# Queries and keys of the last eight heads ahead of their values, and stick-breaking steps one half later

## The chip, the cores and the metric

The kernel runs on one core of a Trainium2 chip. The metric is the device time of one execution in microseconds; times are medians of several executions, and one execution was profiled.

## The reference

Two layers of a hybrid encoder over 256 tokens of width 2048, in float32. Cut to what matters here:

```
xn   = rms_norm(x)
proj = xn @ w_in                        # 16 heads of 128: q, k, v, and 5 forget columns
a: softmax(q1 k1) - lam * softmax(q2 k2), q and k normed in halves of 64, distance bias   (6 heads)
b: stick-breaking: a = exp(log_sigmoid(z) + sum of log_sigmoid(-z) to the right), strict  (5 heads)
c: softmax(q k + cumulated log forget), q and k normed                                    (5 heads)
x    = x + concat(rms_norm(a), rms_norm(b), rms_norm(c)) @ w_out
x    = x + experts(rms_norm(x))         # 16 experts, top 2 within the best of 4 groups
```

## The kernel before, in words

All engines run long programs of their own, in order, and meet at semaphores. The attention part of a layer is one stream of weights: 96 halves of the input projection and 32 of the output projection (a half is 1024 columns times 128 rows of weights, 12 matmuls; eight halves make a block of 512 output columns). The matmuls work on a sum of two reduced-precision parts. For half n ScalarE writes the high part wh (cut, L522), VectorE the low part wl (cut, L1091), and TensorE does xh·wh, xh·wl and xl·wh (L775 to L777). There are four buffers of wh and wl: the cut of half n + 3 begins when TensorE is through with half n - 1.

The attention of the 16 heads is threaded between the halves. Heads go in the order a b c a b c ... a. Tables made from one row of numbers, TURN, say after which half each step of a head stands: turn (transposes of queries and keys, L826), one half later query (to SBUF) and scores (L844 to L854), then SOFT (row_max, or stick_scores on ScalarE with its table load), EXPS, WEIGH (weigh or stick_keep, VectorE, L1255 to L1260), MIDDLE (transposes of the weights, or the cumulated sum of a stick-breaking head, L869 to L878), BACK and SUMMED, STICK (stick_weights, L1272), OUTPUT (weights times values, L892 and L894) and OUT (ScalarE copies and squares, L606, L607). At step n each engine first does its cut of half n + 3 (TensorE: half n itself) and then the steps that the tables give to n, VectorE in the order to_proj (L1197), stick_weights, stick_sum, head_norms, turned_lo, row_max, stick_keep or weigh, out_norms. TensorE's order at a step is output, middle, scores, turn, mixed group.

When a block of eight halves is done, to_proj (first step of the next block) copies it to proj; one step later ScalarE squares the queries and keys in it (head_squares, L623), two steps later VectorE norms them (head_norms: a chain of small operations from L1099 and a scaling at L1144). A turn waits for the norms of its block. out_norms does the same to a pair of head outputs; the mixed groups (turn_group, L789, with turned_hi at L534 and turned_lo at L1128) transpose them for the output projection. In the last four heads the columns stand in another order: all their queries and keys, then all their values, and their outputs come at steps 96 to 99.

Of the kernel before, what the change touches and what calls it, by code (L numbers as in the profile page):

```python
# [24 lines left out]
P = 128  # L25
D, SEQ, DEPTH = 2048, 256, 2
NT = SEQ // P
NC = D // P
HD = 128
NH = D // HD  # L30
# [34 lines left out]
NORMS = NORM_AT[NH]  # L65
LATE = NH - 4
Q_AT = [3 * HD * i if i < LATE else 3 * HD * LATE + 2 * HD * (i - LATE) for i in range(NH)]
K_AT = [q + HD for q in Q_AT]
V_AT = [3 * HD * i + 2 * HD if i < LATE else 3 * HD * LATE + HD * (8 + i - LATE) for i in range(NH)]
SPAN = P + SEQ  # L70
# [28 lines left out]
NORMED = {j: [i for i in range(NH) if QK_BLOCK[i] == j and KIND[i] != "b"] for j in range(IN_UNITS // 4 - 1)}  # L99
TURN = dict(zip((19, 23, 27, 31, 36, 43, 51, 55, 59, 67, 75, 79, 83, 86, 90, 92), range(NH)))  # L100
BEGIN = {i: n for n, i in TURN.items()}


def steps_at(after, late=None):

    at = {}
    for i, n in BEGIN.items():
        n += after[KIND[i]] if isinstance(after, dict) else after
        if late is not None and i >= LATE:
            n = late + i - LATE  # L110
        at.setdefault(n, []).append(i)
    return at
# [5 lines left out]
WEIGH = steps_at(4)  # L118
MIDDLE = steps_at(5)
BACK = steps_at({"a": 6, "b": 7, "c": 6})  # L120
SUMMED = steps_at(6)
STICK = steps_at(8)
OUTPUT = steps_at({"a": 6, "b": 8, "c": 6}, IN_HALVES)
OUT = steps_at({"a": 7, "b": 9, "c": 7}, IN_HALVES + 1)
PAIR = {max(n for n, h in OUT.items() if 2 * g in h or 2 * g + 1 in h) + 1: g for g in range(NH // 2)}
MIXED = {91: 0, 92: 1, 93: 2, 94: 3, 97: 4, 98: 5, 100: 6, 101: 7}
MIX_BANK = (0, 1, 0, 1, 2, 3, 2, 3)
# [166 lines left out]
def trunk(nc, x_in, in_units, forget_w, out_units, expert_units, norms, small_in, const_in, router_in,  # L294
          rows_dram, picks_dram, out):
    with ExitStack() as ctx:
# [31 lines left out]
        rx = sb("rx", [P, NT])  # L328
        gains = sb("gains", [P, 2, NC])
        out_stat = sb("out_stat", [P, 3, NT, NH])  # L330
        more = sb("more", [1, 2])
# [24 lines left out]
        def sml(name):  # L356
# [16 lines left out]
                   for b in range(2)]  # L373
        weights = [wT[:, i % 2, :] if i < NH - 2 else proj[:, i % 2, 0:SPAN] for i in range(NH)]
        squares = wide[:, 4 * SPAN:4 * SPAN + NT * 2 * HD]
        turned_qk_bank, score_bank, middle_bank = bank[4], (bank[5], bank[6]), bank[7]
        out_bank = [(middle_bank if i < LATE else turned_qk_bank)[:, 0:NT * HD] for i in range(NH)]
        turned_w = wT[:, :, :].rearrange("p a n -> p (a n)")
# [130 lines left out]
        def _(e):  # L509
# [39 lines left out]
            with t_.layers():  # L549
# [38 lines left out]
                def turned(i):  # L588
                    if KIND[i] == "b":
                        e.wait_ge(S["sum_ready"], t_.due("sum_ready"))  # L590
                        act_(score[:, i % 2, 1, :], score[:, i % 2, 1, :], ACT.Exp).then_inc(S["a_ready"], 1)
                        return
                    e.wait_ge(S["m_banked"], t_.by("m_banked", i + 1))
                    if 2 <= i < NH - 2:

                        e.wait_ge(S["o_banked"], t_.by("o_banked", i - 1))
                    act_(weights[i], middle_bank[:, 0:SPAN], ACT.Copy).then_inc(S["wT_ready"], 1)

                def output(i):
                    e.wait_ge(S["o_banked"], t_.by("o_banked", i + 1))  # L600
                    if KIND[i] == "c":
                        e.wait_ge(S["sums_ready"], t_.due("sums_ready"))
                    for t in range(NT):
                        scale = soft[:, i % 3, 3, 2 * t:2 * t + 1] if KIND[i] == "c" else 1.0
                        o = out_bank[i][:, t * HD:(t + 1) * HD]
                        act_(rows[:, t, i * HD:(i + 1) * HD], o, ACT.Copy, scale=scale)  # L606
                        last = act_(o, o, ACT.Square, scale=scale,  # L607
                                    accum_out=out_stat[:, 0, t, i:i + 1])
                    last.then_inc(S["o_ready"], 1)
# [17 lines left out]
                def during(n):  # L627
# [25 lines left out]
                    for i in steps(TURN, n - 1):  # L653
                        query(i)
                    if n - 1 in MIXED:
                        turned_hi(MIXED[n - 1], mix_gain, MIX_BANK[MIXED[n - 1]])
                    for i in EXPS.get(n, ()):
# [109 lines left out]
        def _(e):  # L767
# [114 lines left out]
            def output(i):  # L882
                at, w = V_AT[i], weights[i]
                if i == LATE:

                    e.wait_ge(S["block_out"], t_.ahead("block_out", 1))
                if KIND[i] == "b":
                    at_least("aT_ready", KIND[:i + 1].count("b"))
                else:
                    at_least("wT_ready", i + 1 - KIND[:i].count("b"))  # L890
                at_least("o_ready", i)
                mm(out_bank[i][:, 0:HD], w[:, 0:P], proj[:, 0, at:at + HD], start=True, stop=True)  # L892
                for u in range(NT):
                    last = mm(out_bank[i][:, HD:2 * HD], w[:, (1 + u) * P:(2 + u) * P],  # L894
                              proj[:, u, at:at + HD], start=(u == 0), stop=(u == 1))
                last.then_inc(S["o_banked"], 1)
# [80 lines left out]
            with t_.layers():  # L977
# [42 lines left out]
                for n in range(4, HALVES):  # L1020
# [12 lines left out]
                    for i in steps(TURN, n):  # L1033
                        turn(i)
                    if n in MIXED:
                        g = MIXED[n]
                        at_least("mix_scaled", g + 1)
# [45 lines left out]
        def _(e):  # L1083
# [78 lines left out]
            with t_.layers() as layer:  # L1162
# [104 lines left out]
                def stick_weights(i):  # L1267
                    e.wait_ge(S["a_ready"], t_.due("a_ready"))
                    if i >= 2:

                        at_least("o_banked", i - 1)
                    v.tensor_tensor(weights[i], score[:, i % 2, 1, :], strict, ALU.mult).then_inc(S["aT_ready"], 1)  # L1272
# [34 lines left out]
                def weigh(i):  # L1307
                    b, m = i % 2, i % 3
                    e.wait_ge(S["exps_ready"], t_.due("exps_ready"))
                    if KIND[i] == "c":  # L1310
                        v.reciprocal(soft[:, m, 3, 0:3:2], soft[:, m, 2, 0:3:2]).then_inc(S["sums_ready"], 1)
                        return
# [15 lines left out]

                def out_norms(g):

                    at_least("o_ready", 2 * g + 2)
                    k = slice(2 * g, 2 * g + 2)
                    inverse_root(out_stat, 2 * g, 2 * g + 2, {HD: (2 * g, 2 * g + 2)})
                    for t in range(NT):
                        ins = scaled_heads(rows[:, t, 2 * g * HD:(2 * g + 2) * HD], out_stat[:, 2, t, k], 2)
                    ins.then_inc(S["mix_scaled"], 1)
                    if g == NH // 2 - 1:

# [3 lines left out]
                def during(n):  # L1342
# [24 lines left out]
                    if n % 8 == 2 and n // 8 - 1 in NORMED:  # L1367
                        head_norms(n // 8 - 1)
                    if n - 1 in MIXED:
                        turned_lo(MIXED[n - 1], mix_gain, MIX_BANK[MIXED[n - 1]])  # L1370
                    for i in SOFT.get(n, ()):
                        if KIND[i] != "b":
                            row_max(i)
                    for i in WEIGH.get(n, ()):
                        if KIND[i] == "b":
                            stick_keep(i)
                        else:
                            weigh(i)
                    for g in steps(PAIR, n):
                        out_norms(g)  # L1380
                    if n > HALVES - 8 and n - HALVES + 7 < 6:
# [302 lines left out]
```

## Time and profile before

| | us |
|---|---|
| median of 3 runs | 2129.95 (2129.71 to 2131.52) |
| the profiled execution | 2122.7 |
| its span, first to last instruction | 2121.0 |
| TensorE, VectorE, ScalarE busy | 1884.9, 1597.2, 1436.7 |
| mean granted clock of TensorE | 0.954 |

Each layer has three parts: the two projections with the attention between their halves, the routing, and the experts. A busy time is a sum over the span, so it mixes these parts; the tables of windows tell them apart. A clock of 1.00 is 2.4 GHz, 0.50 is 1.2 GHz. "[4.40 <-DVE proj L1144]" behind a row means that the engine was idle for 4.40 us before it, and that VectorE's instruction at L1144 ended the wait.

### The profile page before, as it was taken

Reading aid. Unit: us, or ns where it says so; the run is one execution under the profiler, and the core shown is the slowest. Engines: PE = TensorE matmul, PEld = TensorE weight load, DVE = VectorE, ACT = ScalarE, POOL = GpSimd, SP = SyncE. Lnnn points to the kernel's source line nnn. Section 1 sums busy time; section 2 is a strip of 40 time slices with the busy share of each in tenths; the row PEclk is TensorE's granted clock in tenths of the full one; section 3 lists DMA queues with packets and bytes.
Section 4 is the critical chain, followed back from the end, with each engine's and each line's share of the span. In section 5 each row is a group of like instructions: output and inputs, shape, how many; then the busy total and the mean of one; then the engine's idle time right before and its main releaser. Section 6 shows DMA issues by size and latency. Waiting matters only on the chain.

```text
span 2121.0 us, 31136 instructions
## 1 busy us (share of the span) xinstructions
PE 1884.9 (89%) x8974; PEld 1484.9 (70%) x8974; DVE 1597.2 (75%) x2301; ACT 1436.7 (68%) x2278; POOL 92.2 (4%) x86
## 2 busy tenths in 40 slices
PE   7999998995999999999489999989869999999993
PEld 6877776784677777677377777767757777677772
DVE  5567676546999999999464676665579999999993
ACT  5555555433888988989355555654448988988982
POOL 0000000001000000000000000000010000000000
PEclk9999999996999999999789999999879999999996
DMA  6434343454999999999534344435569999999993
GB/s 259 159 139 158 142 158 119 175 203 151 394 398 405 402 400 413 396 408 407 230 141 141 138 159 152 153 115 188 189 210 407 404 403 404 402 406 397 405 381 138
DMA packets 83005, 575.14 MB, mean 271 GB/s; under 512 B 11760, under 2 KB 12016, under 8 KB 13264
## 3 DMA queue, kind: packets, MB, share of 16 engines
q1 hardware_dynamic: 75600, 542.01, 66.0%
q0 software_dynamic: 7296, 31.85, 4.3%
q8 instruction: 48, 0.79, 0.2%
q14 instruction: 61, 0.50, 0.1%
HBM read 567.52 MB, written 23.07 MB: 278 GB/s over the span
## 4 chain that ended last, share of the span: by engine, by line
PE 64%; ACT 11%; issue 11%; DVE 9%; DMA 3%; ACTq 1%; DVEq 0%; POOLq 0%; POOL 0%; SPq 0%
PE bank L775 9%; PE bank L777 9%; PE bank L776 9%; PE bank L940 6%; ACT wh L522 6%; PE bank L924 6%; PE bank L942 6%; PE bank L941 6%; PE bank L926 5%; DVE wl L1091 3%; PE bank L907 2%; ACT rows L719 2%; PE bank L915 1%; DMA proj<-picks 1%; ACT wT L706 1%
## 5 line engine op out<-in xcount | busy, mean ns | idle before, releaser
L1091 DVE TENSOR_TENSOR wl<-raw,wh 128x1024 fp32r<-128x1024 f32 x640 | 767.7, 1222 | 325.8 <-ACT wh L522 324.9
L522 ACT ACTIVATE wh<-raw 128x1024 fp32r<-128x1024 f32 x640 | 664.3, 1054 | 407.4 <-PE bank L777 341.0
L1091 DVE TENSOR_TENSOR wl<-proj,wh 128x1024 fp32r<-128x1024 f32 x384 | 455.3, 1221 | 46.6 <-ACT wh L522 46.1
L924 PE MATMUL bank<-wh,xh 128*128 128x512 f32 x1024 | 428.0, 418 | 32.4 <-DVE wl L1091 29.4
L522 ACT ACTIVATE wh<-proj 128x1024 fp32r<-128x1024 f32 x384 | 394.5, 1052 | 66.5 <-PE bank L942 50.1
L775 PE MATMUL bank<-wh,xh 128*128 128x512 f32 x1024 | 418.8, 409 | 5.8 <-DVE xl L1128 3.1
L926 PE MATMUL bank<-wl,xh 128*128 128x512 f32 x1024 | 405.9, 396 | 0.0
L777 PE MATMUL bank<-wh,xl 128*128 128x512 f32 x1024 | 404.2, 395 | 0.0
L776 PE MATMUL bank<-wl,xh 128*128 128x512 f32 x1024 | 403.7, 394 | 0.0
L924 PEld LDWEIGHTS bank<-wh,xh 128*128 128x128 f32 x1024 | 194.3, 190 | 120.2 <-DVE wl L1091 80.6
L775 PEld LDWEIGHTS bank<-wh,xh 128*128 128x128 f32 x1024 | 195.8, 191 | 49.1 <-DVE wl L1091 9.5
L777 PEld LDWEIGHTS bank<-wh,xl 128*128 128x128 f32 x1024 | 194.9, 190 | 43.6
L776 PEld LDWEIGHTS bank<-wl,xh 128*128 128x128 f32 x1024 | 195.8, 191 | 37.0
L926 PEld LDWEIGHTS bank<-wl,xh 128*128 128x128 f32 x1024 | 194.9, 190 | 34.1
L940 PE MATMUL bank<-wh,actT 128*128 128x512 f32 x512 | 209.7, 410 | 3.6 <-DVE actT L1527 3.6
L942 PE MATMUL bank<-wh,actT 128*128 128x512 f32 x512 | 203.2, 397 | 0.0
L941 PE MATMUL bank<-wl,actT 128*128 128x512 f32 x512 | 203.2, 397 | 0.0
L940 PEld LDWEIGHTS bank<-wh,actT 128*128 128x128 f32 x512 | 96.8, 189 | 38.4 <-DVE wl L1091 11.2
L942 PEld LDWEIGHTS bank<-wh,actT 128*128 128x128 f32 x512 | 96.8, 189 | 23.1
L941 PEld LDWEIGHTS bank<-wl,actT 128*128 128x128 f32 x512 | 97.1, 190 | 19.7
L915 PEld LDWEIGHTS bank<-const,wT 128*128 128x128 f32 x512 | 66.1, 195 | 43.7 <-ACT wT L706 40.3
L915 PE MATMUL bank<-const,wT 128*128 128x64 f32 x512 | 69.1, 279 | 27.3 <-ACT wT L706 27.3
(209 smaller groups left out, 1539.0 us busy)
## 6 DMA issues: line engine op xcount, KB each, us to landing
raw<-in_expert_units SPq DMA_DIRECT2D x192, 1024.0 KB, 9.2
proj<-in_expert_units SPq DMA_DIRECT2D x192, 1024.0 KB, 9.4
raw<-in_in_units SPq DMA_DIRECT2D x96, 1024.0 KB, 4.8
raw<-in_out_units SPq DMA_DIRECT2D x32, 1024.0 KB, 4.8
proj<-picks POOLq DMA_DIRECT2D x8, 1024.0 KB, 8.1
expert_rows<-rows POOLq DMA_DIRECT2D x4, 1024.0 KB, 4.3
x<-in_x SPq DMA_DIRECT2D x2, 1024.0 KB, 6.4
wide<-in_norms POOLq DMA_DIRECT2D x2, 1024.0 KB, 5.3
```

The source lines that it names most:

```text
L522: act_(wh[:, h % CUT, :], ring[j][:, h % 2 * HALF:(h % 2 + 1) * HALF], ACT.Copy)\
L719: ins = act_(expert_out[b][:, k * COLS:(k + 1) * COLS], bank[2 + k][0:SLOTS, :], ACT.Copy, scale=slots[0:SLOTS, bass.ds(n, 1), 2:3].rearra ...
L775: mm(out, xh[:, at, tok], rh, start=start, stop=False)
L776: mm(out, xh[:, at, tok], rl, start=False, stop=False)
L777: return mm(out, xl[:, at, tok], rh, start=False, stop=stop)
L915: last = mm(bank[6][:, at + k * SLOTS:at + (k + 1) * SLOTS], wide_act[:, k * P:(k + 1) * P], cst("fold"), start=True, stop=True)
L924: mm(bank[m][:, :], stacked[b][:, 2 * h + c, :], wh[:, j, k], start=(h + c == 0), stop=False)
L926: last = mm(bank[m][:, :], stacked[b][:, 2 * h + c, :], wl[:, j, k], start=False, stop=(h == PART - 1 and c == 1))
L940: mm(o, actT[:, k, 0:STACK], wh[:, j, r], start=(k == 0), stop=False)
L941: mm(o, actT[:, k, 0:STACK], wl[:, j, r], start=False, stop=False)
L942: last = mm(o, actT[:, k, SLOTS:SLOTS + STACK], wh[:, j, r], start=False, stop=(k == 3))
L1091: v.tensor_tensor(wl[:, h % CUT, :], ring[(first + h // 2) % slots][:, h % 2 * HALF:(h % 2 + 1) * HALF], wh[:, h % CUT, :].bitcast(F32), A ...
```

## The change

LATE goes from NH - 4 to NH - 8: the columns of the last eight heads (8 to 15) now stand as their queries and keys first and then their values, in blocks 10 and 11. TURN is another row of numbers: heads 2 and 8 are turned one half later, heads 9 to 15 between four and eight halves earlier. The middle, sum, weights and output of a stick-breaking head come one half later after its turn. The outputs of heads 8 to 15 come at steps 89, 90, 91, 92, 96, 96, 97 and 97; their weights lie in dead columns of proj until then, and their outputs go to banks 4 to 7. The inverse sums of the forgetting heads get a tile of their own, inv_sum. out_norms can take several pairs, and pairs 6 and 7 go together, as do their mixed groups (step 100). In the table of steps:

| | before | after |
|---|---|---|
| turn of heads 0 to 7 | 19 23 27 31 36 43 51 55 | 19 23 28 31 36 43 51 55 |
| turn of heads 8 to 15 | 59 67 75 79 83 86 90 92 | 60 63 67 71 75 78 84 87 |
| block of q and k, heads 8 to 15 | 6 7 8 8 9 9 10 10 | 6 6 7 7 8 8 9 9 |
| middle, stick_weights and output of a stick head, after its turn | 5, 8, 8 | 6, 9, 9 |
| out_norms of pairs 0 to 7 | 33 39 51 65 75 87 99 101 | 34 39 51 66 92 94 99 99 |

```diff
-LATE = NH - 4
+LATE = NH - 8
-V_AT = [3 * HD * i + 2 * HD if i < LATE else 3 * HD * LATE + HD * (8 + i - LATE) for i in range(NH)]
+V_AT = [3 * HD * i + 2 * HD if i < LATE else 3 * HD * LATE + HD * (2 * (NH - LATE) + i - LATE) for i in range(NH)]
-TURN = dict(zip((19, 23, 27, 31, 36, 43, 51, 55, 59, 67, 75, 79, 83, 86, 90, 92), range(NH)))
+TURN = dict(zip((19, 23, 28, 31, 36, 43, 51, 55, 60, 63, 67, 71, 75, 78, 84, 87), range(NH)))
+LATE_OUTPUT = (89, 90, 91, 92, 96, 96, 97, 97)
...
-            n = late + i - LATE
+            n = LATE_OUTPUT[i - LATE] + late
...
-MIDDLE = steps_at(5)
-BACK = steps_at({"a": 6, "b": 7, "c": 6})
-SUMMED = steps_at(6)
-STICK = steps_at(8)
-OUTPUT = steps_at({"a": 6, "b": 8, "c": 6}, IN_HALVES)
-OUT = steps_at({"a": 7, "b": 9, "c": 7}, IN_HALVES + 1)
-PAIR = {max(n for n, h in OUT.items() if 2 * g in h or 2 * g + 1 in h) + 1: g for g in range(NH // 2)}
-MIXED = {91: 0, 92: 1, 93: 2, 94: 3, 97: 4, 98: 5, 100: 6, 101: 7}
+MIDDLE = steps_at({"a": 5, "b": 6, "c": 5})
+BACK = steps_at({"a": 6, "b": 8, "c": 6})
+SUMMED = steps_at(7)
+STICK = steps_at(9)
+OUTPUT = steps_at({"a": 6, "b": 9, "c": 6}, 0)
+OUT = steps_at({"a": 7, "b": 10, "c": 7}, 1)
...
+PAIR[max(PAIR)] = [6, 7]
+PAIR = {n: (g[0], g[-1] + 1) for n, g in PAIR.items() if g != [6]}
+MIXED = {91: (0,), 92: (1,), 93: (2,), 94: (3,), 97: (4,), 98: (5,), 100: (6, 7)}
...
-        weights = [wT[:, i % 2, :] if i < NH - 2 else proj[:, i % 2, 0:SPAN] for i in range(NH)]
+        weights = [wT[:, i % 2, :] if i < LATE
+                   else proj[:, i % 2, (i - LATE) // 2 * SPAN:((i - LATE) // 2 + 1) * SPAN] for i in range(NH)]
...
-        out_bank = [(middle_bank if i < LATE else turned_qk_bank)[:, 0:NT * HD] for i in range(NH)]
+        out_bank = [middle_bank] * LATE + [bank[m] for m in (4, 6, 4, 6, 4, 6, 5, 7)]
...
-                    if 2 <= i < NH - 2:
+                    if 2 <= i < LATE:
...
-                if i == LATE:
+                if i in (LATE, LATE + 4):
 
                     e.wait_ge(S["block_out"], t_.ahead("block_out", 1))
...
-                at_least("o_ready", i)
+                at_least("o_ready", i if i < LATE else i - 1)
+                if i >= LATE:
+
+                    at_least("neg_max", HA + HC)
+                    at_least("z_ready", HB)
...
-                        at_least("o_banked", i - 1)
+                        at_least("o_banked", min(i - 1, LATE))
...
-                        v.reciprocal(soft[:, m, 3, 0:3:2], soft[:, m, 2, 0:3:2]).then_inc(S["sums_ready"], 1)
+                        v.reciprocal(inv_sum[:, HEADS[i][1], :], soft[:, m, 2, 0:3:2])\
+                            .then_inc(S["sums_ready"], 1)
...
-                def out_norms(g):
+                def out_norms(first, end):
 
-                    at_least("o_ready", 2 * g + 2)
-                    k = slice(2 * g, 2 * g + 2)
-                    inverse_root(out_stat, 2 * g, 2 * g + 2, {HD: (2 * g, 2 * g + 2)})
-                    for t in range(NT):
-                        ins = scaled_heads(rows[:, t, 2 * g * HD:(2 * g + 2) * HD], out_stat[:, 2, t, k], 2)
-                    ins.then_inc(S["mix_scaled"], 1)
+                    at_least("o_ready", 2 * end)
+                    inverse_root(out_stat, 2 * first, 2 * end, {HD: (2 * first, 2 * end)})
+                    for g in range(first, end):
+                        k = slice(2 * g, 2 * g + 2)
+                        for t in range(NT):
+                            ins = scaled_heads(rows[:, t, 2 * g * HD:(2 * g + 2) * HD], out_stat[:, 2, t, k], 2)
+                        ins.then_inc(S["mix_scaled"], 1)
```

ScalarE's sigmoid in the experts stands in both kernels; the diff does not touch it.

## Rows read from the trace of the kernel before

**Rows 1.** The page's first line

```profile
span 2121.0 us, 31136 instructions
```

**Rows 2.** Busy time by window: layers' attention, plain halves, experts (clock, DMA share, GB/s last)

```profile
103.60:393.10 289.50, 265.42 (x1271) 214.15 (x1270) 194.19 (x456) 165.53 (x438) 0.54 (x1) 0.97 0.41 145
1161.90:1448.70 286.80, 262.78 (x1257) 212.01 (x1256) 194.26 (x456) 162.88 (x421) 0.53 (x1) 0.97 0.40 142
404.01:436.65 32.64, 32.64 (x145) 27.03 (x144) 15.91 (x15) 12.73 (x12) 0.00 (x0) 1.00 0.55 194
600.00:1000.00 400.00, 378.20 (x1770) 285.90 (x1771) 372.45 (x359) 357.81 (x435) 29.06 (x23) 1.00 1.01 403
```

**Rows 3.** Timeline of TensorE's weight loads, first layer: start, us, line, [idle before]

```profile
113.34 0.72 PEld L826 LDWEIGHTS bank<-const,proj 128*128 128x128 f32 x4 [4.40 <-DVE proj L1144]
...
165.68 0.30 PEld L869 LDWEIGHTS bank<-wide,const 128*128 128x128 f32 x2 [2.61 <-DVE wide L1260]
...
225.07 0.42 PEld L826 LDWEIGHTS bank<-const,proj 128*128 128x128 f32 x4 [1.50 <-DVE proj L1144]
...
240.78 0.30 PEld L892 LDWEIGHTS bank<-proj,wT 128*128 128x128 f32 x2 [1.53 <-DVE wT L1272]
...
254.17 0.42 PEld L826 LDWEIGHTS bank<-const,proj 128*128 128x128 f32 x4 [0.90 <-DVE proj L1144]
...
306.93 0.30 PEld L892 LDWEIGHTS bank<-proj,wT 128*128 128x128 f32 x2 [2.12 <-DVE wT L1272]
...
338.47 0.72 PEld L826 LDWEIGHTS bank<-const,proj 128*128 128x128 f32 x4 [7.84 <-DVE proj L1144]
...
362.70 0.19 PEld L775 LDWEIGHTS bank<-wh,xh 128*128 128x128 f32 x1 [1.78 <-DVE wl L1091]
...
366.01 0.30 PEld L892 LDWEIGHTS bank<-proj,wT 128*128 128x128 f32 x2 [0.72 <-DVE proj L1197]
...
387.41 0.72 PEld L789 LDWEIGHTS bank<-const,rows 128*128 128x128 f32 x4 [3.51 <-DVE rows L1144]
```

**Rows 4.** Windows behind waits of 7.84, 3.51, 2.61 (both layers) and 2.12

```profile
338.40:344.30 5.90, 5.83 (x25) 4.99 (x26) 2.74 (x5) 1.59 (x3) 0.00 (x0) 0.70 0.06 25
387.40:394.00 6.60, 6.59 (x19) 5.37 (x20) 1.97 (x3) 1.32 (x3) 0.49 (x1) 0.56 0.78 273
...
165.60:169.20 3.60, 3.52 (x20) 3.07 (x20) 3.46 (x9) 0.64 (x1) 0.00 (x0) 1.00 0.53 178
1222.40:1226.00 3.60, 3.53 (x13) 3.15 (x14) 3.46 (x9) 0.62 (x1) 0.00 (x0) 0.53 0.44 155
306.90:312.00 5.10, 5.07 (x33) 4.20 (x33) 1.17 (x2) 2.63 (x9) 0.00 (x0) 1.00 0.56 177
```

**Rows 5.** Timeline of ScalarE: first square of a block, and the cut behind the squares

```profile
164.01 0.31 ACT L623 ACTIVATE wide<-proj 128x128 f32<-128x128 f32 x1 [2.14 <-DVE proj L1197]
...
165.19 1.04 ACT L522 ACTIVATE wh<-raw 128x1024 fp32r<-128x1024 f32 x1
...
329.00 0.31 ACT L623 ACTIVATE wide<-proj 128x128 f32<-128x128 f32 x1 [1.72 <-DVE proj L1197]
...
332.24 1.99 ACT L522 ACTIVATE wh<-raw 128x1024 fp32r<-128x1024 f32 x2
```

**Rows 6.** Timeline of VectorE: to_proj, stick_keep, two cuts, norms (start and scaling)

```profile
162.57 1.40 DVE L1197 TENSOR_SCALAR proj<-bank,rx 128x512 f32<-128x512 f32 x2
...
163.89 0.55 DVE L1255 SCALAR_TENSOR_TENSOR wide<-wide 128x384 f32<-128x384 f32 x1
...
165.54 2.35 DVE L1091 TENSOR_TENSOR wl<-raw,wh 128x1024 fp32r<-128x1024 f32 x2
...
221.87 0.17 DVE L1099 TENSOR_SCALAR stat<-stat 128x4 f32<-128x4 f32 x1
...
224.26 0.76 DVE L1144 TENSOR_TENSOR proj<-proj,stat 128x256 f32<-128x256 f32 x2
...
336.98 1.43 DVE L1144 TENSOR_TENSOR proj<-proj,stat 128x256 f32<-128x256 f32 x4
```

More of the change, by code:

```diff
@@ L118 @@
 WEIGH = steps_at(4)
-MIDDLE = steps_at(5)
-BACK = steps_at({"a": 6, "b": 7, "c": 6})
-SUMMED = steps_at(6)
-STICK = steps_at(8)
-OUTPUT = steps_at({"a": 6, "b": 8, "c": 6}, IN_HALVES)
-OUT = steps_at({"a": 7, "b": 9, "c": 7}, IN_HALVES + 1)
-PAIR = {max(n for n, h in OUT.items() if 2 * g in h or 2 * g + 1 in h) + 1: g for g in range(NH // 2)}
-MIXED = {91: 0, 92: 1, 93: 2, 94: 3, 97: 4, 98: 5, 100: 6, 101: 7}
+MIDDLE = steps_at({"a": 5, "b": 6, "c": 5})
[4 more added lines that the diff above has]
+OUT = steps_at({"a": 7, "b": 10, "c": 7}, 1)
+PAIR = {}
+for _g in range(NH // 2):
+    PAIR.setdefault(max(n for n, h in OUT.items() if 2 * min(_g, 6) in h or 2 * _g + 1 in h) + 1, []).append(_g)
+PAIR[max(PAIR)] = [6, 7]
+PAIR = {n: (g[0], g[-1] + 1) for n, g in PAIR.items() if g != [6]}
+MIXED = {91: (0,), 92: (1,), 93: (2,), 94: (3,), 97: (4,), 98: (5,), 100: (6, 7)}
 MIX_BANK = (0, 1, 0, 1, 2, 3, 2, 3)
@@ L329, in trunk @@
         gains = sb("gains", [P, 2, NC])
+        inv_sum = sb("inv_sum", [P, HC, NT])
         out_stat = sb("out_stat", [P, 3, NT, NH])
@@ L603, in output @@
                     for t in range(NT):
-                        scale = soft[:, i % 3, 3, 2 * t:2 * t + 1] if KIND[i] == "c" else 1.0
+                        scale = inv_sum[:, HEADS[i][1], t:t + 1] if KIND[i] == "c" else 1.0
                         o = out_bank[i][:, t * HD:(t + 1) * HD]
@@ L654, in during @@
                         query(i)
-                    if n - 1 in MIXED:
-                        turned_hi(MIXED[n - 1], mix_gain, MIX_BANK[MIXED[n - 1]])
+                    for g in MIXED.get(n - 1, ()):
+                        turned_hi(g, mix_gain, MIX_BANK[g])
                     for i in EXPS.get(n, ()):
@@ L1034, in _ @@
                         turn(i)
-                    if n in MIXED:
-                        g = MIXED[n]
+                    for g in MIXED.get(n, ()):
                         at_least("mix_scaled", g + 1)
@@ L1327, in weigh @@
                     ins.then_inc(S["weights_ready"], 1)
-                def out_norms(g):
-                    at_least("o_ready", 2 * g + 2)
-                    k = slice(2 * g, 2 * g + 2)
-                    inverse_root(out_stat, 2 * g, 2 * g + 2, {HD: (2 * g, 2 * g + 2)})
-                    for t in range(NT):
-                        ins = scaled_heads(rows[:, t, 2 * g * HD:(2 * g + 2) * HD], out_stat[:, 2, t, k], 2)
-                    ins.then_inc(S["mix_scaled"], 1)
-                    if g == NH // 2 - 1:
+                def out_norms(first, end):
[6 more added lines that the diff above has]
+                        ins.then_inc(S["mix_scaled"], 1)
+                    if end == NH // 2:
                         e.sem_inc(S["gain_free"], 1)
@@ L1368, in during @@
                         head_norms(n // 8 - 1)
-                    if n - 1 in MIXED:
-                        turned_lo(MIXED[n - 1], mix_gain, MIX_BANK[MIXED[n - 1]])
+                    for g in MIXED.get(n - 1, ()):
+                        turned_lo(g, mix_gain, MIX_BANK[g])
                     for i in SOFT.get(n, ()):
@@ L1378, in during @@
                             weigh(i)
-                    for g in steps(PAIR, n):
-                        out_norms(g)
+                    if n in PAIR:
+                        out_norms(*PAIR[n])
                     if n > HALVES - 8 and n - HALVES + 7 < 6:
```

## The prediction

> **What bounds the kernel now.** I read the page first, then the table of windows, then the waits of the weight loads in order of time, then the two engines that feed them. The span is 2121.0 us [rows 1]. In the experts (the 400 us sample) the DMA share is 1.01 at 403 GB/s: that stage waits for memory, and nothing in the diff touches it. In the projection stages DMA is at 0.40, TensorE is busy for 265.4 of 289.5 us, VectorE for 194 and ScalarE for 166 [rows 2]. Where no attention work lies between, twelve halves take 32.64 us, so one half (12 matmuls) is 2.72 us. The stage is TensorE's, and time can only come from the places where it stands still or runs slowly.
>
> Those places are single rows [rows 3]; the number in brackets is the wait before the first weight load of an attention step, and each row can be placed by counting halves of twelve matmuls (half 27 is the 28th of the layer):
>
> after half 27, 4.40 (turn of head 2, for head_norms); after 31 and 63, 1.53 each (output of heads 1 and 7, for stick_weights; one row stands for both); 41, 2.61 (middle of head 4, for stick_keep); 59, 1.50 and 67, 0.90 (turns of heads 8 and 9); 83, 2.12 (output 10); 90, 7.84 (turn 14, for the norms of heads 14 and 15); 95, 1.78 (half 96, for mixed columns); 96, 0.72 (output 12, for to_proj); 101, 3.51 (mixed group 7, for out_norms).
>
> Sum: 4.40 + 3.06 + 2.61 + 1.50 + 0.90 + 2.12 + 7.84 + 1.78 + 0.72 + 3.51 = 28.4 us a layer. The second layer's stretch has the same busy times and clock [rows 2], so I double.
>
> **The clock.** After the wait of 7.84 the granted clock is 0.70 over 5.9 us, after that of 3.51 it is 0.56 over 6.6 us [rows 4]: stretches partly at 1.2 and partly at 2.4 GHz. That is 0.30 x 5.9 = 1.8 and 0.44 x 6.6 = 2.9 us; with 1.8 taken for the wait of 4.40 too, 6.5 us. Part of such a stretch is transposes and issue that the clock doesn't pace, so I take 5.0, with 6.5 and 3 as ends. Before: 28.4 + 5.0 = 33.4 us a layer. The wait of 2.61 is at the edge: behind it the clock was 1.00 in the first layer and 0.53 over 3.6 us (1.7 lost) in the second, behind that of 2.12 it was 1.00 [rows 4].
>
> **The change part by part.** The number of matmuls, of weight cuts, of norms and of activations stays as it is, but for one chain of norms fewer at the end (pairs 6 and 7 share one inverse root). No queue of SP or POOL is passed: the weight stream is the same, in another column order; POOL's load of the norm gain has waited long before its semaphore comes and nothing needs it until the router. Everything therefore lies in where a step stands against the half that it follows. I walk the new table and ask at each hand-off which queue is last.
>
> Prices: ScalarE's cut 1.05, starting about 0.4 after TensorE has freed the buffer; squares of a forgetting head 1.2 (164.01 to 165.19), of a forgetting and a differential one together 3.2 (329.00 to 332.24) [rows 5]. VectorE: cut 1.15 to 1.22, to_proj 1.3, stick_keep 1.65, norms of one head 2.4 + 0.76 = 3.15, of two 0.8 more [rows 6]. The other steps are estimates from these: weigh and row_max of a differential head four or so passes of 0.56 each, 1.7 and 2.2; a turn or a mixed group 0.55 of TensorE beyond a half, a middle 0.4 (stick 0.85).
>
> - *Turn 2, from 27 to 28.* Its norms end where they did, just before 113.34 [rows 3]; TensorE does one more half first: 4.40 - 2.72 = **1.7** is left.
> - *Outputs 1 and 7, from 31 and 63 to 32 and 64.* stick_weights moves along, but these steps are multiples of 8, where VectorE has to_proj first: 1.53 + 1.3, less the turn now ahead of it (0.55): **2.3** each, a loss.
> - *Middle 4, from 41 to 42.* stick_keep ends at 165.63; TensorE was there at 163.07 and comes now at 165.8: no wait. But what was late goes on: VectorE does two cuts to 167.9 and head_norms to 171.0, and TensorE wants turn 5 at 165.8 + 0.85 + 2.72 = 169.4: **1.6**.
> - *Turn 8, from 59 to 60.* Head 9's queries now share its block: squares +2.0, norms +0.8, one half more of time: 1.50 + 2.8 - 2.72 = **1.6**.
> - *Turn 9, turn 10.* The wait at 67 goes (one plain head in the block, turned at 71, 75). But step 66 gives VectorE head_norms and out_norms: cut 1.15 + 3.15 + 3.15 + cut 1.15 + weigh 1.7 = 10.3, beginning 1.5 after half 65, so middle 9 (step 68) is free at 11.8, where TensorE arrives at 3 x 2.72 + 0.4 + 0.55 = 9.1: **2.6**.
> - *Output 10* moves from 83 to 91, long after its weights: 0.
> - *Turn 14, from 90 to 84, its norms from 90 to 82.* The pattern around steps 80 to 84 is the old one of 88 to 92, without out_norms before to_proj: ScalarE's squares waited 1.72 for that [rows 5], so the chain is 1.7 earlier. stick_keep 13 ends at 336.98 + 1.35 + 1.65 - 1.7 = 338.3 on the old scale; TensorE comes from 330.63 + 2 x 2.72 = 336.1. **2.2** before middle 13, and turn 14 follows without a wait. This is the largest term: 7.84 becomes 2.2.
> - *Output 8 at 89* is new here and waits for row_max 15 (its bank is shared with the scores): half 88's end + 0.4 + 1.05 + 1.2 + 2.2 = 4.9 against scores 1.15 + 2.72 = 3.9: **1.0**. Behind it on TensorE stand middle 14 and half 90, who have slack on their own inputs.
> - *Half 96* waits for mixed group 3, behind out_norms of pair 5: 1.5 + 1.15 + 0.9 + 3.15 + 1.15 + 0.9 = 8.7 against 2 x 2.72 + 1.1 = 6.5, so 2.2 at most; turned columns may be earlier: **2.0**. The 0.72 for to_proj behind it is covered.
> - *Groups 6 and 7 at 100.* First pair ready 1.5 + 1.15 + 0.9 + 3.15 = 6.7 after half 98, TensorE there at 6.0: **0.7** instead of 3.51.
> - *inv_sum* replaces a slot of three by one per head: same instruction, 0; bounds 0 and 0.
>
> New: 1.7 + 2.3 + 1.6 + 1.6 + 2.3 + 2.6 + 2.2 + 1.0 + 2.0 + 0.7 = 18.0 a layer, none above 2.7. Gain 33.4 - 18.0 = 15.4 a layer, 30.8 in two. Of the ten new waits of 2.0 to 2.6 in both layers I let two fall on the low clock, as one of the two old ones of 2.61 did: 2 x 1.7 = 3.4 back, a gain of 27.4 (bounds: none, and all ten). What follows is a memory-bound stage that starts when this one ends, so it passes through whole. Profiled execution: 2122.7 - 27.4 = 2095.3; the median of the runs is 7.25 higher: 2129.95 - 27.4, **2102.5 us**.
>
> **A rule against it.** What the rows show: the waits of 3.51 and 7.84 were followed by low clock, one of the two of 2.61, and not that of 2.12 [rows 3, 4]. The Trainium skill (TensorE: Matmul & The Clock Gate, HAM oscillation) says that waits between bursts of matmuls send the array back to half clock and that every burst then starts cold. By that rule each of my new waits near 2.3 would cost as the old large ones did, which is the first rival; by the rows alone two in ten is my reading.
>
> **Rivals.**
> 1. *All new waits bring the low clock.* The five of 2.0 to 2.6 at 1.7 each [rows 4]: 5 x 1.7 x 2 = 17 us back instead of 3.4: 2116. For it: the second 2.61. Against: the first, and the 2.12. 0.15.
> 2. *Turn 14 keeps its wait.* If the norms at 82 are as late as those at 90 (squares not freed by the shorter VectorE queue, a keep behind them), 84 costs 2.2 + 1.7 + low clock 1.8 and 68 grows as well by such a step of 2.7: 2 x 6 to 8: about 2116. 0.12.
> 3. *Slower: VectorE becomes the bound of halves 60 to 84.* Six heads' softmax steps, three blocks' norms, three to_proj and 25 cuts are, at the prices above, some 64 us in 80. If in-order waits between the engines turn this into a backlog, each of the steps 64, 68, 73, 75, 80 and 84 loses one more half of 2.72 and the clock with it: 6 x (2.72 + 1.7) = 27 against a gain of 15.4: +11 a layer, 2153. It decides from 2.6 us more per such step. Against: TensorE sets the pace in the old stage with VectorE at 0.67. 0.05.
> 4. *It does nothing for the time*: every wait only moves (as 41 to 43 nearly does), the gain is below 4 us: 2126 to 2130. 0.06.
> Forecast: 0.62, own range 2093 to 2110.
>
> **Numbers.** Low end: clock loss 6.5 instead of 5.0 and a quarter of the new waits not there (4.5): 6 a layer, and no low clock, 2087; I take 2089. High end holds rivals 1 and 2: 2118. Under 0.2% (4 us) a measurement here doesn't tell a change. Faster 0.90, same 0.05, slower 0.05.
>
> **What would show it.** In the changed kernel: no wait of a turn for head_norms over 2 us in either layer; a wait before middle 9 and middle 13 near 2.5; outputs 1 and 7 waiting 2.3; half 96 still waiting about 2; mixed groups under 1; the granted clock of the stage at 0.99 or more where it was 0.97; the stage from half 27 to 103 about 14 us shorter than 286.8; the experts unchanged. Wrong if the waits for stick_keep or weigh exceed 4 us (rivals 1 and 2), or if weight cuts (wl) begin to end TensorE's waits in halves 60 to 84 (rival 3).

## The result and the profile after

The changed kernel took 2109.4 us in the median of four executions (2106.8 to 2113.2) against 2130.2 for the kernel before beside it: ratio 0.9912, 95% interval 0.9895 to 0.9929. Six more executions of the same code, measured later beside eleven of before, gave 2110.6 against 2125.7: 0.9931 (0.9913 to 0.9948). The gain is 15 to 21 us; 27.4 was forecast (2102.5 us), so the time came out 7 us above the forecast, inside its range. The profiled execution has a span of 2105.5 us.

The waits of TensorE's weight loads in the first layer of the changed kernel, in order of time (start, us, line, idle before; line numbers are some 10 higher than in [rows 3]):

```profile
113.12 0.42 PEld L835 LDWEIGHTS bank<-const,proj 128*128 128x128 f32 x4 [1.70 <-DVE proj L1156]
...
130.14 0.30 PEld L905 LDWEIGHTS bank<-proj,wT 128*128 128x128 f32 x2 [2.35 <-DVE wT L1284]
...
167.44 0.31 PEld L835 LDWEIGHTS bank<-const,proj 128*128 128x128 f32 x3 [1.62 <-DVE proj L1156]
...
223.35 0.42 PEld L835 LDWEIGHTS bank<-const,proj 128*128 128x128 f32 x4 [1.68 <-DVE proj L1156]
...
240.38 0.30 PEld L905 LDWEIGHTS bank<-proj,wT 128*128 128x128 f32 x2 [2.36 <-DVE wT L1284]
...
256.54 0.31 PEld L887 LDWEIGHTS bank<-const,wide 128*128 128x128 f32 x3 [2.85 <-DVE wide L1337]
...
310.10 0.30 PEld L878 LDWEIGHTS bank<-wide,const 128*128 128x128 f32 x2 [2.26 <-DVE wide L1272]
...
331.41 0.30 PEld L905 LDWEIGHTS bank<-proj 128*128 128x128 f32 x2 [1.20 <-DVE soft L1315]
...
355.18 0.19 PEld L784 LDWEIGHTS bank<-wh,xh 128*128 128x128 f32 x1 [2.26 <-DVE wl L1103]
...
373.37 0.42 PEld L798 LDWEIGHTS bank<-const,rows 128*128 128x128 f32 x4 [1.04 <-DVE rows L1156]
```

They are, in order: turn 2, output 1, turn 5, turn 8, output 7, middle 9, middle 13, output 8, half 96, mixed group 6. The sum is 19.3 us where the waits of [rows 3] had 28.4. The wait of 7.84 is gone and the largest is 2.85. The wait before output 8 ends on L1315, which is row_max, as the prediction said. Against the walk of the prediction (1.7, 2.3, 1.6, 1.6, 2.3, 2.6, 2.2, 1.0, 2.0, 0.7) no term is off by more than 0.35.

Two stretches of each layer are compared from here on. "The stage" is the attention stage from the start of half 27 to that of half 103. "The opening" is the start of the experts, the 16 gate and up halves of the first expert (the expectations below call them its first 16 gate halves). Windows of the changed kernel, the stage in both layers and then the opening in both; third from the end of a row is the clock:

```profile
106.00:379.85 273.85, 258.66 (x1257) 209.01 (x1256) 189.58 (x433) 163.46 (x422) 0.54 (x1) 0.99 0.42 149
1150.23:1425.61 275.38, 260.14 (x1257) 209.97 (x1256) 189.60 (x433) 163.61 (x422) 0.54 (x1) 0.99 0.41 149
491.70:522.30 30.60, 29.75 (x144) 22.52 (x144) 19.95 (x26) 18.42 (x21) 1.86 (x2) 0.72 0.52 182
1537.10:1570.36 33.26, 32.35 (x144) 24.50 (x144) 20.01 (x26) 18.44 (x21) 1.86 (x2) 0.66 0.49 170
```

The same openings in the kernel before:

```profile
505.15:534.84 29.69, 28.80 (x144) 21.48 (x145) 19.99 (x26) 18.34 (x21) 2.37 (x2) 0.76 0.49 172
1561.10:1586.17 25.07, 23.69 (x144) 17.93 (x144) 19.88 (x26) 18.45 (x21) 2.40 (x2) 0.94 0.59 206
```

The stage is 286.8 - 273.85 = 12.9 and 286.8 - 275.4 = 11.4 us shorter, 24.4 together before rounding (in the first layer the same stretch of before, 106.25 to 393.02, is 286.8 us too). But the two spans differ by 15.5 only. What is missing is in the openings: the work is the same in number, 30.6 + 33.3 = 63.9 us after against 29.7 + 25.1 = 54.8 before, and the time goes with the clock, 0.94 to 0.66. That is 9.1 us given back. Nothing else moved: the span less the two stages and the two openings is 1492.6 us before and 1492.4 after, and 1491.7 to 1495.1 in all 13 profiles of this document.

### The profile page after: what moved, and what is told of

Same layout as the page of the kernel before. It is cut to its first block, busy times and chain, and to the rows that moved or that the text cites. A ratio compares the mean times of both kernels' runs of the same rounds, so it can differ in the third digit from the quotient of the medians.

```text
span 2105.5 us, 31034 instructions
## 1 busy us (share of the span) xinstructions
PE 1888.7 (90%) x8974; PEld 1487.9 (71%) x8974; DVE 1588.4 (75%) x2255; ACT 1439.7 (68%) x2278; POOL 91.3 (4%) x86
## 4 chain that ended last, share of the span: by engine, by line
PE 64%; ACT 11%; issue 11%; DVE 10%; DMA 3%; ACTq 1%; DVEq 0%; POOLq 0%; POOL 0%; SPq 0%
PE bank L784 9%; PE bank L786 9%; PE bank L785 8%; PE bank L953 6%; PE bank L937 6%; ACT wh L531 6%; PE bank L955 6%; PE bank L954 6%; PE bank L939 5%; DVE wl L1103 3%; PE bank L920 2%; ACT rows L728 2%; PE bank L928 1%; DMA proj<-picks 1%; ACT wide L632 1%
```

## The experiments

Every kernel ran beside the kernel before on the same chip, the first four on one, the next four on a second, the last three on a third. The kernel before had medians of 2129.0, 2126.8 and 2125.7 us there, so times from different chips can be compared only to some 3 to 4 us.

**One part alone: heads 0 to 6.** The kernel before with

```diff
-TURN = dict(zip((19, 23, 27, 31, ...
+TURN = dict(zip((19, 23, 28, 31, ...
+        if later and i in (1, 4):
+            n += 1
```

for the tables of middle, sum, back, stick, output and out.

> The kernel before with the change's steps of heads 0 to 6 alone: turn of head 2 after half 28 instead of 27, middle, sum, weights and output of heads 1 and 4 one half later. Theory (the change is a sum of single waits on TensorE, each counted where it stands): from half 27 to half 47 a layer takes 72.7 us as in the changed kernel instead of 77.1, so 4.4 us a layer; nothing else moves: 8 to 9 us less than before, 2121 us. Rival (the waits of this part only pass on, the later steps take them up again): within 3 us of before.

2124.6 against 2129.0, ratio 0.9971 (0.9957 to 0.9984). The waits of this part are as in the changed kernel (turn 2 at 1.68, output 1 at 2.35, turn 5 at 1.60, none before middle 4, where before had 4.40, 1.53, none and 2.61), those behind it as before (1.54, 1.53, 0.90, 2.11, 7.82). So the waits don't pass on. Its stages are 281.2 and 281.5 us, 11.0 shorter together than before: 5.8 of that are the waits, the rest is clock. But its openings took 30.6 and 33.2, and the median gain is 4.4 us, half of what was expected.

**The other part alone: heads 7 to 15.** The changed kernel with the old steps of heads 0 to 6 (the reverse of that diff).

> The changed kernel with heads 0 to 6 at their old steps: the new order of columns and the steps of heads 7 to 15 alone. Theory (sum of waits): from half 47 to half 103 a layer is 8.5 us shorter, 17 us in two, 2113 us, and with the part of heads 0 to 6 it adds up to the 20 us of the whole. Rival (one part makes the other useless): 20 us by itself or under 12.

2118.6 against 2129.0, ratio 0.9954 (0.9940 to 0.9968): 10.4 us instead of 17. Its waits fell by 12.7 us in two layers, but its stages, 283.0 and 281.3 us, are only 9.3 shorter together: nine stretches of low clock lie in them, where before has six. So the clock took back 3 us of what its waits gave. In the waits the parts add up (5.8 + 12.7 = 18.5 us, 18.2 in the whole change). In the medians they do within the noise: 0.29% and 0.46% against 0.7 to 0.9%.

**TensorE kept busy through the routing, before and after.**

```diff
+                def keep_warm(count):
+                    for _ in range(count):
+                        mm(bank[3][:, :], ident, const[:, 0:COLS], start=True, stop=True)
...
                 last.then_inc(S["r_banked"], 1)
+                keep_warm(7)
...
                     list_slots(range(FIRST))
+                    keep_warm(9)
```

> The kernel before, and in each layer's routing TensorE does 16 extra matmuls (128x512 float32, into bank 3, results unused) while it waits: 7 before the rank matmuls, 9 before the gathered rows are turned. Theory (what the change lost again at the start of the experts is the low clock there, whose end falls by chance a few us earlier or later): the granted clock is 1.00 when the experts begin, their first 16 halves of gate weights take under 27 us in both layers instead of 25.0 and 29.7, the kernel gets 8 to 18 us faster (2112 to 2122) and its runs lie closer together. Rival (the experts wait for memory from their start, the clock there costs nothing): no change, within 3 us.

> The changed kernel with the same 16 extra matmuls a layer. Theory (clock at the start of the experts takes the missing part of the gain): the difference between this and the kernel before with the same filling is the 24.4 us by which the two attention stages are shorter, give or take 3, and the experts' first 16 halves of gate weights take under 27 us instead of 30.6 and 33.2: about 2092. Rival (a shorter attention stage leaves the experts a longer start for another reason, such as fewer weights loaded ahead): the difference stays at 15 to 20 us whatever the clock.

Before filled: 2126.1 (2121.0 to 2132.3), ratio 0.9985 (0.9975 to 0.9995); after filled: 2105.6, ratio 0.9895 (0.9880 to 0.9909). Their difference is 20.5 us, below what the theory gave (24.4, give or take 3) and just above the 15 to 20 of its rival. The filling did not do what it was for. Windows of the changed kernel, filled: the two filled stretches of the first layer's routing, the first 5.7 us of the opening, the 10 us around its middle, and both whole openings:

```profile
466.86:474.00 7.14, 7.12 (x14) 2.66 (x12) 6.48 (x25) 5.41 (x6) 0.54 (x1) 0.84 0.35 147
481.00:491.50 10.50, 10.50 (x20) 4.26 (x19) 5.17 (x8) 0.00 (x0) 3.38 (x2) 0.75 0.65 206
494.26:500.00 5.74, 5.73 (x51) 4.62 (x52) 4.50 (x4) 3.06 (x3) 0.00 (x0) 0.99 0.00 1
500.00:510.00 10.00, 10.00 (x43) 7.58 (x42) 3.95 (x4) 3.45 (x4) 0.00 (x0) 0.50 0.60 211
494.26:522.26 28.00, 26.86 (x144) 20.28 (x144) 19.79 (x26) 18.34 (x21) 2.39 (x2) 0.82 0.54 192
1536.94:1566.37 29.43, 28.48 (x144) 21.36 (x144) 19.96 (x26) 18.32 (x21) 2.39 (x2) 0.77 0.53 188
```

The experts now begin at full clock (0.99), and six microseconds later, with TensorE busy throughout, it is at 0.50, that is 1.2 GHz. What TensorE did just before and in that stretch, among the wide matmuls, is the slot lists of four experts after each of the halves 1 to 3 and of two after half 4: about a microsecond each time of matmuls of 4 columns. In the other filled kernel the stage of attention is 286.9 and 286.7 us, as in [rows 2], while its openings are 32.2 and 32.3 us: the stage of the kernel before repeats, its openings don't. (That profile is of one of the slowest of its 12 executions, 2132.1 us against a median of 2126.1.)

The lists alone don't bring the low clock. In the second layer of the kernel before, whose opening of 25.1 us starts at 1561.1, three of its four stretches of lists lie in this window, and the clock stays full:

```profile
1566.00:1576.00 10.00, 10.00 (x76) 7.88 (x75) 6.64 (x8) 6.33 (x7) 0.00 (x0) 1.00 0.54 206
```

**The order of VectorE's steps.** stick_weights ahead of to_proj:

```diff
+                    for i in STICK.get(n, ()):
+                        if KIND[i] == "b":
+                            stick_weights(i)
                     if n % 8 == 0 and 8 <= n <= IN_HALVES:
                         to_proj(n // 8 - 1)
```

> The changed kernel, where VectorE does stick_weights ahead of to_proj at a step that has both (64 and 32; the order of two independent pieces of work). Theory (a new wait is the sum of what stands before the awaited step in VectorE's own order): the waits of TensorE before the outputs of heads 1 and 7 fall from 2.36 by the 1.3 of to_proj to 1.0 to 1.1 in both layers, the other waits stay within 0.1, 5 us in two layers. Rival (these waits come from ScalarE's late exp): they stay at 2.3.

The waits of outputs 1 and 7, first layer of this kernel:

```profile
129.18 0.30 PEld L905 LDWEIGHTS bank<-proj,wT 128*128 128x128 f32 x2 [1.06 <-DVE wT L1284]
...
238.11 0.30 PEld L905 LDWEIGHTS bank<-proj,wT 128*128 128x128 f32 x2 [1.03 <-DVE wT L1284]
```

From 2.35 by the 1.3 of to_proj, as priced. The median is 2097.9, ratio 0.9875 (0.9856 to 0.9894): the time fell by more than the 5 us of the waits, as far as that can be said with the changed kernel on other chips. The stages are 272.8 and 271.2 us, 5 to 7 less together than the changed kernel's; the rest in the profile is an opening of 25.4 us in the second layer.

**Two out_norms moved.**

```diff
+PAIR = {{66: 70, 94: 97}.get(n, n): g for n, g in PAIR.items()}
```

> The changed kernel, with out_norms of pair 3 at step 70 instead of 66 and of pair 5 at 97 instead of 94. Theory (the waits before middle 9, 2.85, and before half 96, 2.26, are VectorE's out_norms of 3.1 us each in front of the awaited step): both waits go to under 0.3, nothing new above 0.5 comes, 10 us less in two layers: about 2099. Rival (head_norms and the cuts alone make them late): over 1.5 of each is left.

What they stood in front of is seen in VectorE's timeline of the changed kernel, between half 66 and middle 9: the norms of head 11's block, out_norms of pair 3, a cut, and only then weigh of head 9, whose end at 256.5 is where TensorE's wait of 2.85 ends.

```profile
249.80 0.76 DVE L1156 TENSOR_TENSOR proj<-proj,stat 128x256 f32<-128x256 f32 x2
...
252.87 0.76 DVE L1156 TENSOR_TENSOR rows<-rows,out_stat 128x256 f32<-128x256 f32 x2
253.55 1.22 DVE L1103 TENSOR_TENSOR wl<-raw,wh 128x1024 fp32r<-128x1024 f32 x1
254.69 0.17 DVE L1326 RECIPROCAL soft<-soft 128x4 f32<-128x4 f32 x1
...
255.74 0.75 DVE L1337 SCALAR_TENSOR_TENSOR wide<-wide,soft 128x128 f32<-128x128 f32 x2
```

With the moves that wait is gone altogether, and the one before half 96 goes from 2.26 to 0.48, with 1.08 new behind it. The rows of the moved kernel there:

```profile
351.15 0.19 PEld L785 LDWEIGHTS bank<-wh,xh 128*128 128x128 f32 x1 [0.48 <-issue]
...
354.82 0.30 PEld L906 LDWEIGHTS bank<-proj 128*128 128x128 f32 x2 [1.08 <-DVE proj L1210]
```

The new one is output 12 waiting for to_proj, the old 0.72 that the prediction called covered. The median is 2098.3, ratio 0.9865 (0.9844 to 0.9886). That it meets the expected 2099 is luck: the waits fell by 3.6 us a layer, 7 in two, and not by the expected 10, since one stayed at 0.48 and one of 1.08 came. The profile has another 3.5 us from shorter openings (60.4 us together).

**ScalarE's squares ahead of stick_scores**, by moving the two lines of head_squares up.

> The changed kernel, where ScalarE squares the queries and keys of a block ahead of stick_scores at a step that has both (25 and 57). Theory (turns 2 and 8 wait for norms whose squares stand behind 3.1 us of stick_scores): the waits of 1.70 before turn 2 and 1.68 before turn 8 fall under 0.3, the middles of heads 1 and 7 get no wait of their own, 6 to 7 us less in two layers: about 2103. Rival (stick_scores then is what comes late, for stick_keep and middle): the wait moves to middle 1 and 7 with at least 1 us.

A miss. 2111.3, ratio 0.9925 (0.9904 to 0.9946), no better than the changed kernel. Turn 8 waits as it did (1.64), turn 2 even longer, 2.36 where it was 1.70, in both layers:

```profile
115.11 0.34 PEld L835 LDWEIGHTS bank<-const,proj 128*128 128x128 f32 x3 [2.36 <-DVE proj L1156]
...
226.85 0.42 PEld L835 LDWEIGHTS bank<-const,proj 128*128 128x128 f32 x4 [1.64 <-DVE proj L1156]
```

Neither theory was right: the middles got no wait either. VectorE does head_norms after the cut of its step, and ScalarE's side of that cut comes after both squares and stick_scores, whichever is first. Two rows of the same profile show it. VectorE stands still for 6.22 us before that cut, and the norms follow it; and the squares, moved up, now wait 0.56 us themselves for to_proj, which is about what turn 2 lost (0.66):

```profile
102.63 0.31 ACT L632 ACTIVATE wide<-proj 128x128 f32<-128x128 f32 x1 [0.56 <-DVE proj L1209]
...
109.95 1.22 DVE L1103 TENSOR_TENSOR wl<-raw,wh 128x1024 fp32r<-128x1024 f32 x1 [6.22 <-ACT wh L531]
```

The norms are late for all that ScalarE does before the next cut, and an exchange inside of it wins nothing.

**The slot lists at the start of the experts.** Spread, two experts after each of seven halves:

```diff
-LISTED = {h: tuple(range(FIRST + 4 * i, min(NE, FIRST + 4 * i + 4))) for i, h in enumerate((1, 2, 3, 4))}
+LISTED = {h: tuple(range(FIRST + 2 * i, FIRST + 2 * i + 2)) for i, h in enumerate(range(1, 8))}
```

> The changed kernel, with the slot lists of experts 2 to 15 (tiny matmuls of 4 columns) written two experts after each of the halves 1 to 7 of the first expert instead of four after each of 1 to 4. Theory (what is given back at the start of the experts is low clock, held there by the stretch of tiny matmuls): the clock is back at full sooner, the first 16 gate halves take 25 to 28 us in both layers instead of 30.6 and 33.2, up to 8 us less, 2102. Rival (the length of that low stretch is chance and the lists have no part in it): 25 to 33 us as before, no difference in the median beyond 3 us.

Both openings got longer and alike, 35.1 us at a clock of 0.63:

```profile
493.28:528.37 35.09, 34.22 (x145) 25.13 (x145) 20.06 (x26) 18.68 (x21) 1.85 (x2) 0.63 0.44 159
1548.00:1583.09 35.09, 34.24 (x145) 25.13 (x145) 20.09 (x26) 18.68 (x21) 1.85 (x2) 0.63 0.47 160
```

The direction that was expected is wrong. In both layers the clock stays low until 26.3 us after the start of the opening, 2.8 us behind the last of the lists; in the changed kernel's profile it was full again after 20.3 and 22.8 us. But this profile is of the slowest of six executions (2119.4 us, the others 2110.4 to 2116.3), so 35.1 may not be the usual length. The median, 2113.4, ratio 0.9935 (0.9919 to 0.9952), is 3 us above the changed kernel's on other chips, which is no more than chance and chip can make: by the medians the rival, no difference beyond 3 us, is not refuted.

**Both orders, and with them the lists in one piece** (`LISTED = {1: tuple(range(FIRST, NE))}`).

> The changed kernel with the two rearrangements of VectorE's steps together: stick_weights ahead of to_proj, and out_norms of pairs 3 and 5 at steps 70 and 97. Theory (waits on TensorE add up one by one): per layer the waits between half 27 and half 103 are 20.0 - 2.6 - 3.3 = 14 us, about 12 us less than the changed kernel in two layers, 2097. Rival (the medians of the two single kernels, 11 us below the changed one each, add up): 2087.

> The same, and the slot lists of experts 2 to 15 all after half 1 of the first expert, instead of four experts after each of halves 1 to 4. Theory (the tiny matmuls between the halves hold the clock low, as spreading them over seven halves made the opening 35.1 us in both layers): with the lists in one stretch the wide matmuls behind them follow each other sooner, the first 16 gate halves take 25 to 29 us in both layers instead of 25.4 to 33.2, 3 to 8 us less than without it: about 2091. Rival (chance alone decides): 25 to 33, no difference in the median.

Both orders: 2089.0 (2088.3 to 2092.8), ratio 0.9825 (0.9807 to 0.9843), 21.6 below the changed kernel beside it. The waits are 13.8 us a layer, as expected, but the rival's figure is nearer. The stages of this kernel:

```profile
107.18:374.92 267.74, 258.80 (x1258) 209.13 (x1256) 189.55 (x433) 163.12 (x421) 0.53 (x1) 0.99 0.43 153
1145.68:1411.75 266.07, 257.13 (x1257) 207.61 (x1256) 189.56 (x433) 163.11 (x421) 0.53 (x1) 1.00 0.43 154
```

They take 15 to 17 us less than the changed kernel's (549.2 and 550.7 together, below), of which 12.4 are waits; the rest goes with the clock, which in the second layer's stage is never low. The remaining 5 us of the 21.6 are a matter of which executions were profiled: that of this kernel was the slowest of its five, 3.8 us above the median, that of the changed kernel the fastest of its six, 1.2 below. With the lists in one piece 2085.7 (2083.5 to 2088.9), ratio 0.9806 (0.9787 to 0.9825), and the openings of that kernel are equal:

```profile
487.23:515.49 28.26, 26.61 (x144) 20.29 (x144) 19.78 (x26) 18.38 (x21) 2.39 (x2) 0.80 0.51 183
1521.27:1549.62 28.35, 26.69 (x144) 20.37 (x144) 19.81 (x26) 18.38 (x21) 2.38 (x2) 0.80 0.50 183
```

The stages of the two kernels are equal (533.8 us together in both). In the profiles the openings differ by 6.2 us (56.6 together instead of 62.8), in the medians the kernels differ by 3.2, and four of the five executions with the lists in one piece are below all five without. The gain of the medians is at the lower end of the expected 3 to 8. A single opening of 28.3 would fit the rival, chance, too. This is the fastest of all the kernels here, 40 us below before.

**The changed kernel again.**

> The changed kernel once more, unaltered, with a second profile. Theory (the waits are the same to 0.1 us in every execution and the clock is not): the same waits, 20.0 us a layer between halves 27 and 103, another set of low-clock stretches in the stage and another time for the opening of the experts; median 2106 to 2113. Rival (the first four runs were low by chance): median above 2115, gain under 14 us.

2110.6 (2109.5 to 2115.7). The same waits to 0.1 us (20.6 and 20.0, with the small ones), stages and openings of this second profile:

```profile
108.35:383.72 275.37, 260.21 (x1258) 210.20 (x1257) 189.62 (x433) 162.64 (x414) 0.53 (x1) 0.99 0.41 150
1152.61:1427.96 275.35, 260.21 (x1257) 210.21 (x1256) 189.61 (x433) 163.16 (x421) 0.53 (x1) 0.99 0.40 149
493.98:524.67 30.69, 29.82 (x144) 22.59 (x144) 19.96 (x26) 18.42 (x21) 1.85 (x2) 0.72 0.50 180
1539.70:1572.93 33.23, 32.30 (x144) 24.44 (x144) 19.99 (x26) 18.41 (x21) 1.87 (x2) 0.66 0.49 169
```

## Why the prediction was right, and where it was too high

**The bound.** Right. TensorE sets the pace of the stage, each removed wait shortened it, and rival 3 did not come: in halves 60 to 84 no wait above 0.33 us ends on a weight cut, and the kernel before has such waits of 0.33 too.

**The waits, edit by edit.** Right, in place and size: all ten that were listed are there in both layers and no other one above 0.35 us (in the second profile there is one more, of 0.65). Forecast 28.4 to 18.0 a layer, measured 28.4 to 19.3; in two layers 18.2 us instead of 20.8. The largest misses are mixed group 6 (1.04 for 0.7; "mixed groups under 1" was a sign named in advance and is just missed), half 96 (2.26 for 2.0) and middle 9 (2.85 for 2.6, where the prediction's own terms, 11.8 less 9.1, give 2.7). Which term of each was short no run tells. That the wait is VectorE's queue in front of the awaited step is shown for outputs 1 and 7, middle 9 and half 96 by the two kernels that move steps of VectorE; for the other waits it rests on the size coming out. For the turns of heads 2 and 8 the queue that was named (the squares) was only a part of the reason.

**Rival 2** is out: turn 14 has no wait, middle 13 the 2.26 that were walked. **Rival 4** is out too: the gain is 15 to 21 us, not under 4.

**The clock within the stage.** About right in the first profile, somewhat too high over all. Both profiles of the changed kernel: stages of 549.2 and 550.7 us together, against 573.6, a gain of 24.4 and 22.9. Less the waits, 18.2, that leaves 5 to 6 us for the clock, where 2 x 5.0 - 3.4 = 6.6 was taken. Of the ten new waits of 2 us and more, three are followed by low clock in the first profile (middle 13 in the first layer, middle 9 and half 96 in the second) and four in the second (the same and output 1), where two were forecast; rival 1, all ten, is refuted. Two more profiles have the same stage, the filled kernel's and that with the lists spread: there it was five and six of the ten, and the stages took 551.9 and 553.8 us, which leaves 3.5 and 1.6 for the clock. The reason given for taking 5.0 and not 6.5, that the clock doesn't pace transposes, is not borne out either: the four transposes of turn 14 in the kernel before took 1.12 us at low clock, those behind output 10 0.60 at full.

The prediction carried a rule of the Trainium skill (TensorE: Matmul & The Clock Gate, HAM oscillation) over to its waits near 2.3 us. The example of that section has waits of 3 to 5 us between the bursts, longer than any in the changed kernel. Here 29 of the 64 waits of 2.2 to 2.4 us were followed by low clock, over all profiles.

The window behind middle 13, changed kernel:

```profile
310.10:315.00 4.90, 4.90 (x20) 4.34 (x21) 3.82 (x4) 0.84 (x2) 0.00 (x0) 0.65 0.27 80
```

**"It passes through whole."** This step failed, at least in the profiled executions. The experts are bound by memory, but not their first expert: there TensorE is busy for 29.75 of 30.60 us with the DMA share at 0.52, and at low clock it holds everything up, for a stretch that differs between executions. In the 18 openings with the lists as they stood and nothing filled, four lengths come back: 25.1 to 25.4 us (clock 0.94, three times), 29.7 to 29.8 (0.76, three times), 30.6 to 30.7 (0.72, six times) and 33.0 to 33.2 (0.66, six times). The prediction treated them as a constant. In the two profiles it costs 9.1 us. In the medians, stage minus gain is 23.6 - 20.8 = 3 and 23.6 - 15.1 = 8.5 us, or 1.5 and 7 with the mean stage of all four profiles. The step "the median is 7.25 us higher than the profiled execution", which was only carried along, was the sign of it: the profiled execution of before was faster than all but three of 48 others of the same kernel (2120.7 to 2133.0), and its second opening, 25.1, is the shortest of all. So part of the 9.1 us is luck of that one execution. The mean clock, which is on record for every execution, says the same: over 44 executions of the kernel before, the time falls by about 1.6 us with each 0.001 of clock (correlation -0.83), and the profiled one, at 0.954, is at the upper end.

The forecast of 27.4 was 7 to 12 us too high in the medians. 2.6 of that are the waits and up to 5 the clock in the stage; the rest lies in the openings or the noise of the chips.

**What stays open.** Whether the openings of the changed kernel are longer than those of before in the median, or only in the profile that was taken of before. Both profiles of the changed kernel have 30.6 and 33.2, but two other kernels with an untouched opening had one of 25.4 each. The eight other profiles with the lists as they stood and nothing filled average 61.7 us for their two openings. The median of the kernel before is 7.25 us above its profile of 54.8, which would put its own openings near 62 if all of that lies there (an estimate from these numbers: no second profile of that very kernel was taken). By that estimate the change itself would lengthen the openings little, and no run tells why a shorter attention stage should move the openings.

## What to carry to other kernels

A schedule written by hand can be priced before it is run: take the wait in front of each hand-off from the trace, and count what stands before the awaited step in its own engine's queue; here ten of ten waits came within 0.35 us. Then ask the same of the stage behind it before letting a gain pass through: a stage may be bound by memory as a whole and by the slow clock at its start. And don't add a gain to a single profiled execution without asking how usual it is: look where it stands among the times of the others. A step that is awaited should stand ahead of one that isn't, in its own slot or by moving the other one to a later slot; the two such moves together gave as much in the median (21.6 us, 12.4 of it waits) as the whole change.

## What the runs showed of the hardware

- Low clock in the attention stage came only behind a wait of TensorE of 2.2 us or more. Over the 26 stages of 13 profiles it followed none of the 158 waits of 0.7 to 2.1 us, 29 of 64 of 2.2 to 2.4, 11 of 14 of 2.8 to 2.9, 4 of 6 of 3.5, and all 12 of 4.4 and 7.8; of the six of 2.6 it followed two. Which of the waits near 2.3 it follows changes from execution to execution.
- In the opening the clock was often low though TensorE had work all the time: 0.50 with TensorE busy for 10.00 of 10.00 us in the filled kernel, while stretches of matmuls of 4 columns stood between the wide ones. With these stretches behind seven halves the opening was at 0.63 and 35.1 us twice, behind four at 0.66 to 0.94 and 25.1 to 33.2, behind one at 0.80 and 28.3 twice. But in three of the 18 openings with four stretches the clock was full through all of them, so these stretches alone don't decide it. That they prolong the low clock is suggested by these profiles and by the median, 3.2 us lower with one stretch; more than that is not shown.
- Filling TensorE's waits in the routing raised the clock (0.84 over 7.1 us, 0.75 over 10.5), but 6 us into the opening of the first layer it was at 0.50 again.
- Waits of the changed kernel repeat from profile to profile within 0.1 us, low-clock stretches don't, and the executions of one kernel differ by 4.5 to 12.5 us.
